# Attention of a second layer: keys and values of heads 2 to 7 as chained seven-product blocks, and another placing of the first layer's multiply-adds

## Chip, cores and metric

The kernel runs on one core of one Trainium2 chip, and the metric is the time of one execution on the device in microseconds. Lower is better. All of it is float32.

## What is computed

The reference is two networks in a row; the change lies in the second one, which has two layers. Each layer takes 256 latent tokens and 256 context tokens (512 columns in all), 1024 features wide. The part that matters is the attention inside the mixer, cut to its core:

```
ql, kl, vl, ... = in_proj_split(h_l @ w_in)      # latent tokens
qc, kc, vc, ... = in_proj_split(h_c @ w_in)      # context tokens
q, k = apply_rope(...) on latent tokens only
s = q @ k.T * 64 ** -0.5                         # two maps a head
p = softmax(s);  a = p[0] - lam * p[1];  o = a @ v
```

There are 8 heads; each has 128 columns of q, of k and of v, which are products of the tokens with a weight block of 1024 x 128. In the first layer latent and context tokens both have queries. In the second, the last, only the latent tokens have queries, while keys and values still cover all 512 tokens.

## The kernel before

**Tiles.** Tokens lie on the free axis: xnT holds the normed tokens as 8 chunks of 128 features by 512 columns, columns 0 to 255 latent, 256 to 511 context. Weights stream from HBM by DMA, issued by SyncE (SP), into 12 slots of 1024 x 128 (512 KB each). The list of tiles is fixed (weight_tiles); SP goes through it in order and waits, before each tile, until the tile 12 places earlier has been given back. A tile may be empty: it only holds a slot for sums made on the chip.

**The seven products.** Where two neighbouring weight blocks A and B (two heads, say) both meet all 512 columns, the 2 x 2 blocks (4 chunks of features by 4, 256 tokens by 256) can be done with seven products in place of eight, after sums of tokens (t1 to t4, made by DVE) and sums of weights (sums_of_weights at L896 on POOL: four TENSOR_TENSOR of 128x512 at L899 to L904, into two empty slots and over B). Each product is four matmuls of 256 columns for q and k, eight of 128 columns for v. In the first layer heads 2 to 7 are done so, and two gates of the merge: 11 jobs. The steps are named 1, 2, 6, 5, 7, 4, 3. Steps 1, 6, 7 and 4 run up a sum in PSUM bank 4 (X), and after each ScalarE (ACT) copies the bank to its quarter of q, k or v (seven_copied, L1382). Steps 2, 5 and 3 run up bank 5 (Y), and DVE adds that bank to a quarter after steps 2, 7 and 3 (seven_added, L2997 and L3000). Semaphores c_cp and c_ad count copies and adds. A product on X waits for the copy before it, a product on Y for the add before it.

**Units.** Attention runs in units s of one head and 128 queries: 32 in the first layer (4 a head), 16 in the second (2 a head; unit 2h and 2h+1 are head h). In each, PE does: scores (L2155), filler part 0, the turn (transposes, L2167) of the unit before, filler part 1, the value products (L2181) of the unit before, filler part 2. The filler is the making of q, k and v of later heads. Beside it DVE takes the maximum from PSUM (L3011), ACT two exponentials (L1390), DVE mixes the two maps in L3020 to L3025, and ACT copies the turned map (L1007), without which the value products can't start; DVE then scales the output (out_of, L3005).

**Rotation.** Latent q and k are rotated. POOL multiplies four swapped blocks of 32 rows (rotated, L932, after q and k of the head are kept and the head before is rotated), then DVE multiplies and adds (rope, L2847 and L2849), and the scores of the head wait for it. rope(h+1) stands in the last unit of head h (units 3, 7, 11, ... of the first layer; the odd ones of the second). In the second layer it stands after the mixing and before seven_added of part 1 and out_of.

**Second layer's fillers.** For head h+1, during head h, pieces (L2017) makes q (8 matmuls of 256 columns, L2029), k (8 of 512, L2038) and v (32 of 128, L2050) plainly, in 12 portions of which each part of a unit takes two. ACT keeps each whole (keep, L1283). Units 14 and 15 are filled by gates of the merge (L2194). POOL does only rotated(1) to rotated(7) there, then the weight sums of the merge, which is all of seven-product jobs.

**Multiply-adds.** Beside the first layer's attention DVE also sums rows for a later modulation: eight weight tiles of 512 KB, each in two halves of two instructions (row_sums, L2414 and L2416; a half is two instructions of 128x512). ROWS_AT lists the 16 units that take one half each, behind out_of. A tile's slot is given back with its second half. Unit 9 also has a RECIPROCAL of 512 columns (L3041), units 26, 27 and 31 token sums (L2664 to L2672).

## Time and profile before

| | |
|---|---|
| three runs | 2652.55, 2652.28, 2648.11 us; median 2652.28 |
| the profiled execution | 2652.46 us, of which the span of the trace is 2650.7 |
| PE | busy 2607.0 us, 98% |
| DVE, POOL, ACT | 1569.2, 1149.4, 786.9 us |
| chain that ended last | PE 86%, DVE 5%, issue 3%, ACT 2% |
| granted PE clock | 0.996 of full speed |
| first layer's attention, units 4 to 31 | about 878 to 1085 us |
| second layer's attention, all units | about 2108 to 2281 us |

Times are of one profiled execution, in us from the start of its span. A busy PE is not a PE at its peak, since the ends of matmuls are modelled; so lengths of work on PE are read from one start to the next. Each float32 matmul of the program shows as two of PE in the trace.

### The profile page before, as it was taken

Reading aid. Unit: us, or ns where it says so; the run is one execution under the profiler, and the core shown is the slowest. Engines: PE = TensorE matmul, PEld = TensorE weight load, DVE = VectorE, ACT = ScalarE, POOL = GpSimd, SP = SyncE. Lnnn points to the kernel's source line nnn. Section 1 sums busy time; section 2 is a strip of 40 time slices with the busy share of each in tenths; the row PEclk is TensorE's granted clock in tenths of the full one; section 3 lists DMA queues with packets and bytes.
Section 4 is the critical chain, followed back from the end, with each engine's and each line's share of the span. In section 5 each row is a group of like instructions: output and inputs, shape, how many; then the busy total and the mean of one; then the engine's idle time right before and its main releaser. Section 6 shows DMA issues by size and latency. Waiting matters only on the chain.

```text
span 2650.7 us, 39911 instructions
## 1 busy us (share of the span) xinstructions
PE 2607.0 (98%) x15266; PEld 2036.9 (77%) x15266; DVE 1569.2 (59%) x2636; ACT 786.9 (30%) x1812; POOL 1149.4 (43%) x918
## 2 busy tenths in 40 slices
PE   8999999999999999999999999999999999999998
PEld 6779995555555777888778888876666677899998
DVE  1447835777778577767869660126766733666253
ACT  2430103665656333200021210014555422201210
POOL 4018870333323544455425553401221222586885
PEclk9999999999999999999999999999999999999999
DMA  9437667434441132234455522264443321377553
GB/s 284 97 112 201 186 195 181 110 90 112 106 109 42 55 96 72 71 97 120 120 159 175 159 88 88 87 180 121 109 112 98 96 72 56 84 219 215 167 170 118
DMA packets 519310, 333.10 MB, mean 126 GB/s; under 512 B 15328, under 2 KB 485712, under 8 KB 518864
## 3 DMA queue, kind: packets, MB, share of 16 engines
q1 hardware_dynamic: 507888, 298.19, 39.9%
q0 software_dynamic: 10784, 31.46, 4.9%
q8 instruction: 122, 2.00, 0.3%
q10 hardware_dynamic: 448, 0.89, 0.1%
q14 instruction: 68, 0.56, 0.1%
HBM read 328.11 MB, written 2.38 MB: 125 GB/s over the span
## 4 chain that ended last, share of the span: by engine, by line
PE 86%; DVE 5%; issue 3%; ACT 2%; DVEq 1%; POOL 1%; PEld 1%; POOLq 1%; DMA 0%; PEldq 0%; ACTq 0%
PE ps L1859 42%; PE ps L1495 23%; PE ps L2216 2%; PE ps L2013 2%; PE ps L2038 2%; PE ps L2050 2%; PE ps L1990 1%; PE ps L2029 1%; PE ps L2181 1%; PE ps L2155 1%; PE ps L2320 1%; POOL TMP L932 1%; PE ps L1815 1%; DVE TMP L3011 1%; PE ps L1976 0%
## 5 line engine op out<-in xcount | busy, mean ns | idle before, releaser
L1495 PE MATMUL ps<-xnT,W 128*128 128x512 f32 (+1 forms) x1760 | 651.6, 526 | 1.6 <-DVE TMP L2793 0.9
L1495 PEld LDWEIGHTS ps<-xnT,W 128*128 128x128 f32 x1760 | 330.8, 191 | 290.6 <-issue 261.2
L1859 PE MATMUL ps<-TMP,W 128*128 128x128 f32 (+1 forms) x2848 | 482.3, 319 | 3.8 <-DVE TMP L2660 1.7
L899 POOL TENSOR_TENSOR W<-W 128x512 f32<-128x512 f32 x148 | 209.4, 1415 | 595.7 <-DMA W<-in_w_mlp 246.2
L1859 PEld LDWEIGHTS ps<-TMP,W 128*128 128x128 f32 x2848 | 422.9, 191 | 35.8 <-issue 2.4
L1859 PE MATMUL ps<-BIG,W 128*128 128x128 f32 (+1 forms) x2736 | 437.6, 314 | 0.7 <-DVE TMP L2700 0.5
L1859 PEld LDWEIGHTS ps<-BIG,W 128*128 128x128 f32 x2736 | 391.4, 191 | 27.8 <-issue 1.0
L1859 PE MATMUL ps<-xnT,W 128*128 128x128 f32 (+1 forms) x2032 | 324.2, 311 | 0.0
L1859 PEld LDWEIGHTS ps<-xnT,W 128*128 128x128 f32 x2032 | 288.7, 191 | 18.9 <-issue 0.6
L1007 ACT ACTIVATE TMP<-ps 128x512 f32<-128x512 f32 (+3 forms) x217 | 97.8, 457 | 621.8 <-PE ps L1859 409.3
L901 POOL TENSOR_TENSOR W<-W 128x512 f32<-128x512 f32 x148 | 210.4, 1422 | 25.6 <-issue 4.7
L902 POOL TENSOR_TENSOR W<-W 128x512 f32<-128x512 f32 x148 | 216.4, 1462 | 0.0
L904 POOL TENSOR_TENSOR W<-W 128x512 f32<-128x512 f32 x148 | 202.2, 1366 | 21.6 <-issue 0.9
L2793 DVE SCALAR_TENSOR_TENSOR TMP<-ps,prmT,TMP 128x510 f32<-128x510 f32 (+3 forms) x256 | 181.6, 714 | 43.3 <-ACT TMP L1230 28.9
L956 POOL TENSOR_TENSOR BIG<-BIG,TMP 128x512 f32<-128x512 f32 x80 | 103.8, 1312 | 226.9 <-ACT BIG L1272 226.9
L2699 DVE TENSOR_TENSOR TMP<-TMP,ps 128x128 f32<-128x128 f32 (+1 forms) x89 | 29.5, 331 | 282.9 <-PE ps L1859 273.3
L2829 DVE SCALAR_TENSOR_TENSOR TMP<-TMP 128x128 f32<-128x128 f32 x384 | 162.5, 494 | 41.6 <-ACT TMP L1266 41.6
L2416 DVE SCALAR_TENSOR_TENSOR TMP<-W,cact,TMP 128x512 f32<-128x512 f32 x140 | 176.5, 1292 | 6.8
L967 POOL TENSOR_TENSOR TMP<-TMP 128x512 f32<-128x512 f32 (+1 forms) x30 | 30.0, 999 | 280.8 <-ACT TMP L1280 278.7
L1256 ACT ACTIVATE TMP<-BIG,TMP 128x128 f32<-128x128 f32 x384 | 116.8, 389 | 1.5 <-PE ps L2013 1.5
L932 POOL TENSOR_TENSOR TMP<-TMP,cst 32x512 f32<-32x512 f32 x40 | 51.9, 1298 | 131.9 <-ACT TMP L1007 122.7
L1390 ACT ACTIVATE TMP<-ps,TMP 128x512 f32<-128x512 f32 (+1 forms) x96 | 58.3, 612 | 152.5 <-DVE TMP L3011 152.5
(388 smaller groups left out, 3315.2 us busy)
## 6 DMA issues: line engine op xcount, KB each, us to landing
W<-in_w_in SPq DMA_DIRECT2D x188, 512.0 KB, 4.2
W<-in_w_mlp SPq DMA_DIRECT2D x128, 512.0 KB, 4.0
W<-in_ada_w SPq DMA_DIRECT2D x96, 512.0 KB, 4.2
BIG<-cs_rows POOLq DMA_DIRECT2D x96, 256.0 KB, 4.8
W<-in_w_ssd_o SPq DMA_DIRECT2D x32, 512.0 KB, 4.5
W<-in_w_gate SPq DMA_DIRECT2D x22, 512.0 KB, 6.3
W<-in_w_up SPq DMA_DIRECT2D x22, 512.0 KB, 4.0
W<-in_w_down SPq DMA_DIRECT2D x16, 512.0 KB, 3.8
```

What stands on the lines that cost most here:

```text
L899: nc.gpsimd.tensor_tensor(w1[:, 0:K, :], wb[:, 0:K, :], wb[:, K:2 * K, :], ALU.add)
L901: nc.gpsimd.tensor_tensor(wb[:, 0:K, :], wa[:, 0:K, :], wb[:, 0:K, :], ALU.subtract)
L902: nc.gpsimd.tensor_tensor(w1[:, 4:4 + K, :], w1[:, 0:K, :], wa[:, 0:K, :], ALU.subtract)
L904: nc.gpsimd.tensor_tensor(w2[:, 0:K, :], wa[:, K:2 * K, :], w1[:, 4:4 + K, :], ALU.subtract).then_inc(done, 1)
L956: nc.gpsimd.tensor_tensor(e, e, xs[:, 3, ch * P:(ch + 1) * P].unsqueeze(1) .to_broadcast([P, 4, P]), ALU.mult).then_inc(ssd["ec"], 1)
L1007: return A(dst, src, ACT.Copy)
L1256: last = A(mt[:, (2 * c + d) % 4, h, :], csb[:, ch, d, h, :], ACT.Relu, scale=-1.0, bias=tabs[:, 2, ch, span(g * 4 + 32 * d + h, 1)])
L1495: last = mm(dst, w[:, c, 0:m], rhs(k), start=k == 0, stop=k == total - 1)
L1859: done = mm(PS[bank][:, third + half * H:third + half * H + H], w[:, at + c, :], x[:, c, :], start=first and opens and c == 0, stop=last a ...
L2416: last = V.scalar_tensor_tensor(out=dst, in0=w[:, k, :], scalar=c, in1=dst, op0=ALU.mult, op1=ALU.add)
L2793: last = V.scalar_tensor_tensor(out=acc[:, :, lo:hi], in0=raw[:, :, lo + k - 2:hi + k - 2], scalar=tap(l, g, t, k), in1=acc[:, :, lo:hi], ...
L2829: V.scalar_tensor_tensor(out=mt[:, c % 4, h, :], in0=mt[:, c % 4, h, :], scalar=tabs[:, 0, order[i], span(g * 4 + 32 * d + h, 1)], in1=cbm ...
```

## The change

The second layer's k and v of head pairs (2,3), (4,5) and (6,7) become six seven-product jobs; q stays plain (steps 8 and 9, one head each, 8 matmuls of 256 columns on bank X, copied by ACT). The order is written out for units 2 to 13 (the part after the colon is "part 0", "part 1", "part 2"; "2k6" is pair 2, k, step 6). Units 0 and 1 still make head 1 plainly. Waits by formula become waits by position in the written order.

```diff
+SEVEN_JOBS = ... + [(1, p, t) for p in (1, 2, 3) for t in "qkv"]
+ {2: ("1q8 1q9", "1k1 1k2 1k6", "1k5 1k7"), 3: ("1k4 1k3", "1v1 1v2", "1v6 1v5"), 4: ("1v7", "1v4", "1v3"),
+  5: ("2q8", "2q9", "2k1 2k2"), 6: ("2k6", "2k5", "2k7"), 7: ("2k4 2k3", "2v1", "2v2"),
+  8: ("2v6", "2v5", "2v7"), 9: ("2v4 2v3", "3q8", "3q9"), 10: ("3k1 3k2", "3k6 3k5", "3k7"),
+  11: ("3k4 3k3", "3v1", "3v2"), 12: ("3v6", "3v5", "3v7"), 13: ("3v4", "3v3", "")}
-ROWS_AT = (7, 8, 10, 11, 12, 13, 15, 16, 17, 18, 20, 21, 22, 23, 25, 26)
+ROWS_AT = (8, 9, 10, 12, 13, 14, 16, 17, 18, 20, 21, 22, 24, 25, 26, 28)
```

POOL makes the weight sums of k before rotated(h) and those of v after it, for h = 1, 3, 5, in both layers now (in the first, q before and k and v after):

```diff
-                    if l == 0 and h % 2 == 1 and h < 7:
+                    if h % 2 == 1 and h < 7:
                         pool.drain()
-                        sums_of_weights(seven_keys(job_for(h + 1, "q")), 4, c_ws)
+                        sums_of_weights(seven_keys(job_for(l, h + 1, "k" if l else "q")), 4, c_ws)
                         pool.drain()
                     rotated(h)
...
-                        for t in "kv":
-                            sums_of_weights(seven_keys(job_for(h + 1, t)), 4, c_ws)
+                        for t in "v" if l else "kv":
+                            sums_of_weights(seven_keys(job_for(l, h + 1, t)), 4, c_ws)
```

Waits of PE, in scores, values and the products (copies_until and adds_until count the copies or adds up to a step in the written order):

```diff
                     if qt == 0 and paired(l, h):
-                        pe.wait_ge(c_ad, 3 * job_for(h, "k") + 3)
+                        pe.wait_ge(c_cp, copies_until(job_for(l, h, "k"), 4))
+                        pe.wait_ge(c_ad, adds_until(job_for(l, h, "k"), 3))
...
-                        pe.wait_ge(c_cp, 4 * job_for(h, "v") + 4)
-                        pe.wait_ge(c_ad, 3 * job_for(h, "v") + 3)
+                        pe.wait_ge(c_cp, copies_until(job_for(l, h, "v"), 4))
+                        pe.wait_ge(c_ad, adds_until(job_for(l, h, "v"), 3))
...
+                    if step in (1, 6, 7, 4, 8, 9):
+                        pe.wait_ge(kept["att"], 6 * l + 6)
+                        if copies_until(job, step) > 1:
+                            pe.wait_ge(c_cp, copies_until(job, step) - 1)
+                    elif adds_until(job, step) > 1:
+                        pe.wait_ge(c_ad, adds_until(job, step) - 1)
```

DVE makes the second layer's token sums t1 (in unit 0), t2 and t4 (unit 1) and t3 (unit 2), each 128x1024, t1 to t4 in columns of hT and other memory that this layer does not use; the gates of units 14 and 15 wait for all copies and adds. The tile list has two empty tiles more for each of the six jobs.

```diff
-                    if l == 0 and s < 3:
+                    for _ in range((1, 2)[s] if l and s < 2 else 1 if not l and s < 3 else 0):
                         next(seven_sums, None)
```

## Rows read from the trace of the kernel before

**Rows 1.** The page: its span.

```profile
span 2650.7 us, 39911 instructions
```

**Rows 2.** Busy time by engine, second layer's units 0 to 13; last PEclk, DMA share, GB/s.

```profile
2109.00:2266.00 157.00, 157.00 (x886) 113.47 (x882) 54.28 (x96) 42.00 (x117) 38.60 (x32) 1.00 0.22 60
```

**Rows 3.** Timeline of PE, a second-layer odd unit: start, us, instructions xcount [idle before <-releaser].

```profile
2162.44 1.13 PE L2155 MATMUL ps<-TMP 64*128 64x512 f32 x4
2163.50 3.70 PE L2038 MATMUL ps<-xnT,W 128*128 128x512 f32 x8
2167.03 0.60 PE L2167 MATMUL ps<-cst,TMP 128*128 128x128 f32 x4
2167.47 3.74 PE L2050 MATMUL ps<-W,xnT 128*128 128x128 f32 x32
2171.04 1.06 PE L2181 MATMUL ps<-TMP 128*128 128x128 f32 x8
2171.94 3.74 PE L2050 MATMUL ps<-W,xnT 128*128 128x128 f32 x32
2175.60 1.13 PE L2155 MATMUL ps<-TMP 64*128 64x512 f32 x4
```

**Rows 4.** Timeline of PE, first layer: a product of q or k, then of v.

```profile
893.20 1.89 PE L2216 MATMUL ps<-xnT,W 128*128 128x256 f32 x8
894.92 0.60 PE L2167 MATMUL ps<-cst,TMP 128*128 128x128 f32 x4
...
919.70 2.05 PE L2213 MATMUL ps<-W,BIG 128*128 128x128 f32 x16
921.59 0.38 PE L2167 MATMUL ps<-cst,TMP 128*128 128x128 f32 x2
```

**Rows 5.** Timeline of ACT, second layer: the latent tokens' copy, the second exponential.

```profile
2158.22 0.38 ACT L1286 ACTIVATE TMP<-ps 128x256 f32<-128x256 f32 x1 [0.88 <-PE ps L2029]
...
2165.55 0.68 ACT L1390 ACTIVATE TMP<-ps,TMP 128x512 f32<-128x512 f32 x1
```

**Rows 6.** Timeline of DVE, second layer: maximum, mixing, rotation; last two beside POOL's weight sums.

```profile
2163.61 1.23 DVE L3011 TENSOR_REDUCE TMP<-ps 128x2 f32<-128x1024 f32 x1 [3.56 <-PE ps L2155]
...
2166.89 0.75 DVE L3025 SCALAR_TENSOR_TENSOR TMP<-TMP 128x512 f32<-128x512 f32 x1
...
2173.92 0.69 DVE L2849 TENSOR_TENSOR TMP<-TMP 128x512 f32<-128x512 f32 x1
...
2264.51 1.60 DVE L2849 TENSOR_TENSOR TMP<-TMP 128x512 f32<-128x512 f32 x1
...
2266.29 1.49 DVE L2667 TENSOR_TENSOR BIG<-xnT,BIG 128x512 f32<-128x512 f32 x1
```

**Rows 7.** Timeline of POOL: first weight sums of two sets (first layer), rotated rows (second).

```profile
1004.06 1.26 POOL L899 TENSOR_TENSOR W<-W 128x512 f32<-128x512 f32 x1 [7.97 <-PE ps L2216]
...
1055.79 2.09 POOL L899 TENSOR_TENSOR W<-W 128x512 f32<-128x512 f32 x1 [8.21 <-DVE hT L2416]
...
2167.91 5.21 POOL L932 TENSOR_TENSOR TMP<-TMP,cst 32x512 f32<-32x512 f32 x4 [17.42 <-ACT TMP L1007]
```

**Rows 8.** Timeline of PE, first layer: four waits at value products; the merge's third product.

```profile
924.34 0.71 PE L2181 MATMUL ps<-TMP 128*128 128x128 f32 x4 [0.59 <-ACT TMP L1007]
...
939.34 1.16 PE L2181 MATMUL ps<-BIG,TMP 128*128 128x128 f32 x8 [1.07 <-ACT TMP L1007]
...
982.31 0.71 PE L2181 MATMUL ps<-BIG,TMP 128*128 128x128 f32 x4 [1.85 <-ACT TMP L1007]
...
1039.51 0.71 PE L2181 MATMUL ps<-TMP 128*128 128x128 f32 x4 [1.68 <-ACT TMP L1007]
...
1088.85 1.89 PE L1859 MATMUL ps<-TMP,W 128*128 128x256 f32 x8
```

**Rows 9.** Timeline of DVE, first layer: reciprocal, multiply-adds.

```profile
933.85 3.34 DVE L3041 RECIPROCAL TMP<-TMP 128x512 f32<-128x512 f32 x1
...
976.70 2.67 DVE L2416 SCALAR_TENSOR_TENSOR hT<-W,cact,hT 128x512 f32<-128x512 f32 x2
```

More of the change, by code:

```diff
@@ L299, in seven_keys, with seven_of, steps_until, copies_until @@
         pair = [("att", l, 2 * p + i, t) for i in range(2)]
-    return pair + [("sevensums", l, p, t, k) for k in range(2)]
-def seven_of(s, part):
-    return [(SEVEN_JOBS.index((0, int(x[0]), x[1])), int(x[2])) for x in SEVEN_FILL.get(s, ("",) * 3)[part].split()]
+    return pair if (l, t) == (1, "q") else pair + [("sevensums", l, p, t, k) for k in range(2)]
+def seven_of(l, s, part):
+    return [(SEVEN_JOBS.index((l, int(x[0]), x[1])), int(x[2])) for x in SEVEN_FILL[l].get(s, ("",) * 3)[part].split()]
+SEVEN_ORDER = [x for l in range(2) for s in sorted(SEVEN_FILL[l]) for part in range(3) for x in seven_of(l, s, part)]
+def steps_until(kinds, job, step):
+    return sum(x[1] in kinds for x in SEVEN_ORDER[:SEVEN_ORDER.index((job, step)) + 1])
+def copies_until(job, step):
+    return steps_until((1, 6, 7, 4, 8, 9), job, step)
+def adds_until(job, step):
+    return steps_until((2, 5, 3), job, step)
+def copies_of(l):
+    return sum(x[1] in (1, 6, 7, 4, 8, 9) for x in SEVEN_ORDER if SEVEN_JOBS[x[0]][0] <= l)
+def adds_of(l):
+    return sum(x[1] in (2, 5, 3) for x in SEVEN_ORDER if SEVEN_JOBS[x[0]][0] <= l)
 MIXER = ["A0q", "A0k"] + list(WIDE) + [f"A{_i}{_t}" for _i in (1, 2, 3) for _t in "qkv"]
@@ L426, in weight_tiles @@
                     col(("dt", l), wi, SSD_DT, 64)
-        for h in range(8 if l else 2):
+        for h in range(2):
             for n, t in enumerate("qkv"):
@@ L758, in seven_done @@
             if step in (1, 2, 7):
-                eng.wait_ge(c_pe, 3 * job + (1, 2, 7).index(step) + 1)
+                eng.wait_ge(c_pe, steps_until((1, 2, 7), job, step))
+            elif step in (8, 9):
+                made(eng, seven_keys(job)[step - 8])
             else:
@@ L2201, in product_of @@
                     t = SEVEN_JOBS[job][2]
+                    if step in (1, 6, 7, 4, 8, 9):
+                        pe.wait_ge(kept["att"], 6 * l + 6)
[3 more added lines that the diff above has]
+                        pe.wait_ge(c_ad, adds_until(job, step) - 1)
+                    X, Y = PS[4][:, 0:S], PS[5][:, 0:S]
+                    if step in (8, 9):
+                        key = seven_keys(job)[step - 8]
+                        w = tile(key)
+                        for c in range(KC):
+                            last = mm(X, w[:, c, :], xnT[:, c, 0:nt], start=c == 0, stop=c == KC - 1)
+                        give(last, key)
+                        return
                     ka, kb, k1, k2 = seven_keys(job)
@@ L2220, in product_of @@
                     if step == 1:
-                        if job == 0:
-                            pe.wait_ge(kept["att"], 6)
-                        else:
-                            pe.wait_ge(c_cp, 4 * job)
                         tile(ka)
@@ L2254, in filled @@
                     h = us[s][0]
-                    if l == 0 and h:
-                        for job, step in seven_of(s, part):
+                    if h and (l == 0 or h < 7):
+                        for job, step in seven_of(l, s, part):
                             product_of(job, step)
@@ L2262, in _ @@
                 for s, (h, qt, k0, nk) in enumerate(us):
-                    if qt == 0 and (l or h == 0):
-                        ahead = pieces(h + 1) if h < 7 else gate_pieces(0)
+                    if qt == 0 and h == 0:
+                        ahead = pieces(1)
+                    if l and qt == 0 and h == 7:
+                        ahead = gate_pieces(0)
                     scores(s)
@@ L2986, in seven_added @@
                 def seven_added(s, part):
-                    for job, step in seven_of(s, part) if l == 0 else ():
+                    for job, step in seven_of(l, s, part):
                         if step not in (2, 7, 3):
@@ L2991, in seven_added @@
                         seven_done(dve, job, step)
-                        dve.wait_ge(c_cp, 4 * job + {2: 1, 7: 3, 3: 2}[step])
+                        dve.wait_ge(c_cp, copies_until(job, {2: 1, 7: 7, 3: 6}[step]))
                         i, m = {2: (0, 0), 7: (1, 1), 3: (0, 1)}[step]
@@ L3013, in _ @@
                     seven_added(s, 0)
-                    if l == 0 and s == 4:
+                    if s == (2 if l else 4):
                         next(seven_sums, None)
```

68 lines of the change are left out of this document (31 added, 37 removed), and 15 rows, old and new, of the table SEVEN_FILL.

## The prediction

> **What bounds the kernel now.** I read the page first: a span of 2650.7 us [rows 1], most of it PE. Then the busy time by stretch over the units that change: PE has work in all 157 us, DVE in 54, ACT in 42, POOL in 39, at the full granted clock [rows 2]. So in the second layer's attention only fewer columns on PE can save time, and only as long as nothing else makes PE wait. Then PE's timeline, for lengths from start to start. An odd unit runs 13.16 us: scores 1.06, half a k 3.53, the turn 0.44, half a v 3.57, value products 0.90, half a v 3.66, with no wait [rows 3]. So a head's k costs 7.06 and its v 7.23; a pair costs 14.12 and 14.46. The time outside the span in that execution is 1.76 us; its 2652.46 us lies 0.2 above the median of the three runs, 2652.28, so I forecast the median from it directly. Something like 0.2% (5.3 us) is what a measurement of this kernel can tell from no change.
>
> **What the products save.** A product of a k job takes 1.72 us, of a v job 1.89 [rows 4]; behind a change of shape or another product these move by some 0.1 either way, so I take 1.77 and 1.83. Seven make 12.4 and 12.8 in place of 14.12 and 14.46, which is 1.7 + 1.65 = 3.35 a pair and **10.1 us** for three. The q steps have the shapes of before: nothing. New empty tiles bring no DMA; weights of each pair land units ahead, since slots come free with the products of the pair before, and I cost them at nothing: the cover is two units or more, over 15 us.
>
> **What the chain costs.** Each unit now has its own clock. Against a unit's start [rows 3, 5, 6]: DVE's maximum starts at 1.17 and ends 2.40; ACT's second exponential ends at 3.79 and with reading its sum ACT is free at about 3.8, so a copy (0.38) ends at 4.15 at the earliest; DVE's mixing ends at 5.2. Before, ACT copied one k or v in this time; now up to three copies stand in it, and PE stands behind them where two X products have no Y product between.
>
> Unit 2, "1q8 1q9". DVE's token sums t2 and t4 now stand behind rope(1) and ahead of unit 2's maximum, while POOL makes the weight sums of 1v, a set of four such instructions of 1.26 [rows 7], over 5 us. A sum of 512 columns beside POOL took 1.49 [rows 6]; one of 1024 is more than that and less than twice it: 2.0. Both then delay the maximum by about 3.4 against a scores' end where it was waiting: the maximum starts some 4.5 into the unit, the copy of 1q8 comes 3.0 later, at 7.5, and 1q8 had ended at 4.6. **2.9** (ends: 0.6, the copy alone, and 4).
>
> Unit 4, "1v7" and "1v4": 1v7 ends at 2.95, the turn at 3.4, the copy at 4.15: **0.85** with the semaphores. In unit 5 2q9 stands behind 2q8 with only the turn between: 0.2. Other X pairs have 1.7 us of other work between them: nothing, and 0.2 for all.
>
> Rotation. k is kept by ACT at 4.15 in units 3, 7 and 11 (before: at 5.4, since k ended at 4.6). POOL's rotated takes 5.2 [rows 7] and ends at 9.45. rope takes 1.46 alone (0.69 twice and the drain [rows 6]) and 2.37 with POOL's weight sums beside its second multiply, 1.60 in place of 0.69 [rows 6]. Behind rotated(2) POOL goes at once to the sums of 2k, behind rotated(4) to those of 3k; behind rotated(6) it has rotated(7), which waits for rope(6). So the head is rotated at 11.85 in units 3 and 7 and at 10.95 in unit 11. Now the units' lengths, with scores, turn and values 2.4 in sum: unit 3 has six products, 13.3; units 7 and 11 four ("2k4 2k3", "2v1", "2v2"), 9.7. Scores of head 4 wait **2.2**, those of head 6 **1.3**. Unit 3 is long enough, but 1v5 waits for the add of 1v2, which DVE has behind rope(2): 12.3 against 11.45, **0.85**. Unit 5, 9: rotated is early, nothing. The collision of rope(1) makes head 1 0.9 later, of which 0.1 shows.
>
> Unit 13. Its value products are of head 6 and wait for 3v's last add (step 3), which is multiplied just before them, in part 1. On DVE that add stands behind rope(7). PE is ready at 5.2; DVE ends the mixing at 5.2, rope(7) at 6.6, the add at 7.0: **1.85**. Were POOL's first merge sums beside it, 1 to 2 more; by their slots they end by 4 in unit 13.
>
> Sum: 2.9 + 0.85 + 0.2 + 0.2 + 2.2 + 1.3 + 0.85 + 0.1 + 1.85 = **10.4**. The second layer's attention comes out level, +0.3. After it nothing moves: POOL begins the merge's sums as the slots allow, as before.
>
> The Trainium skill (SBUF — State Buffer, section "Who interferes with whom") says that a vector instruction with two SBUF inputs and a GpSimd one that reads SBUF take one shared port as an exclusive lock, and the loser waits out the whole other instruction. The 0.91 us lost [rows 6] are under one instruction of 1.26 [rows 7], so the trace agrees. By that rule t2 and t4 could each wait out 1.26, and unit 2's term would be 3.7 in place of 2.9.
>
> **The first layer.** The halves leave units 7, 11, 15 and 23 and go to 9, 14, 24 and 28. There a half (2.67 beside POOL [rows 9]; alone two instructions of some 0.7, as rope's [rows 6]) stood ahead of the next unit's maximum, and the value products waited for ACT's copy: 0.59 us in unit 8, 1.85 in unit 16, 1.68 in unit 24 [rows 8]. I take all three as gone: -4.1. The unit 11 one showed no wait. In unit 9 the half joins a RECIPROCAL of 3.34 [rows 9] that already makes 1.07 of wait at 939.34 [rows 8]: +1.4. In 14 and 24 DVE has slack; in 28 POOL no longer runs beside it (its sums wait for the slot that this half gives back), so about 0. Weight tiles for which SP waits behind those slots come one unit later (about 8 us), the last two units, 15 us: the merge's first sums, which wait for the last of these slots, began at 1055.8 [rows 7], and PE first uses them at 1088.9 [rows 8]; moved 15 and 5 long, they are still made 12 ahead: nothing. POOL's sums fall on other instructions of DVE: -1 to +2, taken as 0. Net **-2.7**, ends -4.5 and +1.5.
>
> **Total:** 2652.46 + 0.3 - 2.7 = **2650.0**.
>
> **Rivals.**
> 1. Faster: the waits overlap. If the maximum of unit 2 is not held by t2 and t4 (0.6), the rotations are alone (1.3 and 0 in units 7 and 3) and the add comes in time in unit 13 (0.5), the sum is 0.6 + 0.85 + 0.4 + 1.3 + 1.3 + 0.1 + 0.5 = 5.0, and the time 2652.46 - 10.1 + 5.0 - 2.7 = 2644.7. For it: every term is a difference of two chains that I laid out from another unit's rows. Against: in the first layer just such chains made waits [rows 8]. Chance 0.30.
> 2. Slower: the shared port. DVE and POOL hold each other up in both layers. It decides where POOL's sums overlap all of rope, each multiply losing the 0.91 [rows 6]: then units 3 and 7 have 0.9 more each, 11 and 13, where I left POOL out, 1.8 each, unit 2 1, and the moved sums in the first layer eat up its 2.7. Sum 6.4 + 2.7: 2659.1. Against: POOL starts its sums only after DVE's first multiply has begun, and behind rotated(6) it has none to make. Chance 0.11.
> 3. The second layer does as forecast and the first layer's placing brings nothing, since the reciprocal of unit 9 and the half in 28 give back what units 16 and 24 gain: 2652.8. Chance 0.12.
> 4. No wait remains at all, the whole 10.1 + 2.7: 2639.7. The copy behind 1q8 and the add ahead of head 6's values speak flatly against it. Chance 0.03.
> My forecast keeps 0.44.
>
> **How the numbers follow.** Faster by over 0.2% (under 2647.0) are rivals 1 and 4, less a tail of 1 (0.04), plus 0.03 of the forecast: 0.32. Slower (over 2657.6) is most of rival 2 and a small tail of 3: 0.11. Within: 0.57. The likeliest case alone would have 2647 to 2654. The range for 8 in 10 runs from 2643, which takes in rival 1 with a margin of 2 for its terms, to 2656.
>
> **What would show it.** Right: in units 2 to 13 PE's busy time falls by about 10 us and waits of near 10 appear, the largest ahead of 1q9 (line of the plain q products, released by ACT), ahead of the scores in units 8 and 12 (released by DVE's rope) and at the value products of unit 13 (released by DVE's add); in the first layer the waits at the value products of units 16 and 24 are gone and that of unit 10 grows to over 2. Wrong: waits of 5 or less in those units, or POOL's sums overlapping the first multiply of rope, or new waits of the merge for its first weight sums.

## The result, and the profile after

The changed kernel takes 2654.03 us (median of 22 executions, 2650.58 to 2659.37), the kernel before 2650.36 (22 executions, 2645.98 to 2655.37). The ratio is 1.0016, 95% interval 1.0010 to 1.0022: 4.2 us slower (2.7 to 5.8). That is under the 0.2% that I had named as the limit of a measurement, but with this many executions the interval doesn't include 1. A second set of 11 gave 1.0009 (1.0001 to 1.0018), 2.4 us. The sign is the opposite of the one that I forecast (-2.4).

The page of the changed kernel: span, busy time by engine, and the chain that ended last.

```profile
span 2652.7 us, 40131 instructions
PE 2599.8 (98%) x15290; PEld 2047.1 (77%) x15290; DVE 1606.2 (61%) x2658; ACT 788.3 (30%) x1824; POOL 1190.2 (45%) x942
PE 88%; DVE 4%; issue 3%; ACT 2%; DVEq 1%; POOL 1%; PEld 1%; POOLq 0%; PEldq 0%; DMA 0%; ACTq 0%
```

PE is 7.2 us less busy than before, and the span [rows 1] is 2.0 longer. The mean granted clock fell from 0.996 to 0.994. The windows (busy time by engine in a stretch of time) say more. They are laid from one landmark to another: the lines that end at 2290.92 and 2293.79 run from the second layer's first scores to the first product of the merge behind it, the last line of each block from the scores of unit 4 to the same product in the first layer. Columns: length, PE, PEld, DVE, ACT, POOL busy, then the granted clock, the DMA share and GB/s. First the kernel before:

```profile
2108.58:2290.92 182.34, 180.43 (x1012) 132.13 (x1011) 69.98 (x120) 52.35 (x144) 48.77 (x38) 1.00 0.21 58
878.83:1084.95 206.12, 195.30 (x1151) 158.76 (x1151) 139.81 (x224) 69.90 (x241) 95.88 (x71) 1.00 0.26 74
```

and the kernel after:

```profile
2109.00:2266.00 157.00, 147.54 (x896) 121.45 (x894) 80.11 (x112) 43.76 (x129) 79.77 (x58) 0.99 0.24 66
2107.04:2293.79 186.75, 174.86 (x1036) 142.57 (x1035) 96.71 (x142) 54.08 (x156) 85.35 (x62) 0.98 0.23 63
876.67:1082.14 205.47, 196.25 (x1151) 159.96 (x1151) 141.91 (x224) 69.85 (x241) 99.09 (x71) 0.99 0.26 74
```

The first line answers to [rows 2]: where PE had work in all 157 us, it now sits idle for 9.5, and DVE's and POOL's work has grown from 54 and 39 us to 80 each. The second layer's stretch is 4.41 us longer, the first layer's 0.65 shorter. Together +3.76. The spans of the two profiles differ by only 2.0, because outside these stretches, where PE's work is the same, the changed kernel's profile is 1.8 shorter: 2.2 ahead of the first layer's unit 4 and 0.9 behind the second layer, less 1.3 between the two. The executions gave 4.2 and, in the second set, 2.4; I take 3.76 as what the change did in this pair of profiles.

Where PE waits in the second layer (timeline of PE, the lines with idle time before them, and one without; in brackets the us and what ended them). Lines after the change: L2185 is the scores, L2211 the value products, L2244 the plain q, L2258 and L2261 the products of v and of k, L2885 rope's last instruction, L3036 the add.

```profile
2129.33 1.13 PE L2185 MATMUL ps<-TMP 64*128 64x512 f32 x4 [0.48 <-DVE TMP L2885]
2136.68 3.69 PE L2244 MATMUL ps<-xnT,W 128*128 128x256 f32 x16 [2.57 <-issue]
2163.19 2.05 PE L2258 MATMUL ps<-W,hT 128*128 128x128 f32 x16 [1.13 <-DVE BIG L3036]
2165.17 1.13 PE L2185 MATMUL ps<-BIG 64*128 64x512 f32 x4
2169.47 2.02 PE L2258 MATMUL ps<-W,BIG 128*128 128x128 f32 x16 [0.75 <-ACT BIG L1411]
2207.40 2.08 PE L2185 MATMUL ps<-TMP 64*128 64x512 f32 x4 [2.58 <-DVE TMP L2885]
2252.61 1.13 PE L2185 MATMUL ps<-BIG 64*128 64x512 f32 x4 [1.67 <-DVE BIG L2885]
2267.72 1.13 PE L2211 MATMUL ps<-BIG,TMP 128*128 128x128 f32 x8 [1.83 <-DVE BIG L3036]
```

These are the waits that the prediction laid out, nearly one by one. That of 2136.68, ahead of 1q9, the profile puts down to "issue"; what stands ahead of it is ACT's copy of 1q8 (timeline of ACT), which ends at 2136.58:

```profile
2136.20 0.38 ACT L1411 ACTIVATE BIG<-ps 128x256 f32<-128x256 f32 x1
```

But the scores at 2207.40 took 2.08 us where [rows 3] and the line at 2252.61 have 1.13. The windows around them, and around the wait of the first layer's unit 10, show why (last columns again clock, DMA share, GB/s):

```profile
2205.00:2207.40 2.40, 0.00 (x0) 0.00 (x0) 2.33 (x3) 0.00 (x0) 2.00 (x2) 1.00 0.00 0
2207.40:2209.40 2.00, 2.00 (x4) 0.51 (x4) 1.95 (x3) 0.00 (x0) 2.00 (x2) 0.51 0.00 0
2209.40:2212.00 2.60, 2.60 (x19) 2.59 (x18) 1.22 (x1) 1.21 (x3) 2.21 (x3) 0.72 0.00 0
2268.70:2270.70 2.00, 2.00 (x6) 0.45 (x4) 0.95 (x2) 0.00 (x0) 1.86 (x2) 0.54 0.00 0
936.00:938.00 2.00, 0.47 (x2) 0.47 (x3) 1.16 (x3) 2.00 (x8) 1.19 (x1) 0.92 1.11 343
938.00:940.00 2.00, 2.00 (x10) 1.72 (x10) 1.93 (x3) 0.04 (x1) 1.86 (x3) 0.50 0.30 75
```

Behind the wait PE is granted 0.5 of its speed, the lower of its two levels (1.2 in place of 2.4 GHz), and is back at full speed some 3.5 us later. What PE's work loses follows from the rows: 2.00 x 0.49 + 2.60 x 0.28 = 1.7 us. The kernel's time can lose less, when a wait that stood behind gets shorter by it. There are three such stretches in the changed attention (938, 2207, 2269) and none in that of the kernel before.

That is no chance of one profile. Every execution comes with its mean granted clock: over the 22 of the changed kernel it averages 0.9941, over the 27 of the kernel before that were timed beside the last experiments 0.9960. 0.0019 of 2650 us is 5.0 us, three stretches of 1.7. How much of that reaches the time is another question: within each kernel, over the 231 executions whose clock is on record, 0.001 of mean clock goes with some 1.8 us and not with 2.65 (an estimate; the clock is rounded to 0.001, which makes it a little too low).

### The profile page after: what moved, and what is told of

Its sections match the earlier page's. It is cut to its first block, busy times and chain, and to the rows that moved or that the text cites. A ratio compares the mean times of both kernels' runs of the same rounds, so it can differ in the third digit from the quotient of the medians.

```text
span 2652.7 us, 40131 instructions
## 1 busy us (share of the span) xinstructions
PE 2599.8 (98%) x15290; PEld 2047.1 (77%) x15290; DVE 1606.2 (61%) x2658; ACT 788.3 (30%) x1824; POOL 1190.2 (45%) x942
## 4 chain that ended last, share of the span: by engine, by line
PE 88%; DVE 4%; issue 3%; ACT 2%; DVEq 1%; POOL 1%; PEld 1%; POOLq 0%; PEldq 0%; DMA 0%; ACTq 0%
PE ps L1888 42%; PE ps L1524 23%; PE ps L2261 3%; PE ps L2042 2%; PE ps L2258 2%; PE ps L2019 1%; PE ps L2185 1%; PE ps L2211 1%; POOL TMP L961 1%; PE ps L2244 1%; PE ps L2356 1%; PE ps L2058 1%; PE ps L1844 1%; PE ps L2079 1%; PE ps L2067 1%
## 5 line engine op out<-in xcount | busy, mean ns | idle before, releaser
L928 POOL TENSOR_TENSOR W<-W 128x512 f32<-128x512 f32 x154 | 216.9, 1408 | 624.2 <-DMA W<-in_w_mlp 243.2
L1036 ACT ACTIVATE TMP<-ps 128x512 f32<-128x512 f32 (+3 forms) x205 | 91.1, 449 | 579.4 <-PE ps L1888 408.5
L930 POOL TENSOR_TENSOR W<-W 128x512 f32<-128x512 f32 x154 | 219.5, 1425 | 26.8 <-issue 5.2
L931 POOL TENSOR_TENSOR W<-W 128x512 f32<-128x512 f32 x154 | 226.3, 1470 | 0.0
L933 POOL TENSOR_TENSOR W<-W 128x512 f32<-128x512 f32 x154 | 212.1, 1377 | 22.5 <-issue 0.9
L1259 ACT ACTIVATE TMP<-ps,prmT 128x512 f32<-128x512 f32 x64 | 41.8, 653 | 181.1 <-PE ps L1524 181.1
```

What stands on the lines that cost most here:

```text
L928: nc.gpsimd.tensor_tensor(w1[:, 0:K, :], wb[:, 0:K, :], wb[:, K:2 * K, :], ALU.add)
L930: nc.gpsimd.tensor_tensor(wb[:, 0:K, :], wa[:, 0:K, :], wb[:, 0:K, :], ALU.subtract)
L931: nc.gpsimd.tensor_tensor(w1[:, 4:4 + K, :], w1[:, 0:K, :], wa[:, 0:K, :], ALU.subtract)
L933: nc.gpsimd.tensor_tensor(w2[:, 0:K, :], wa[:, K:2 * K, :], w1[:, 4:4 + K, :], ALU.subtract).then_inc(done, 1)
L1036: return A(dst, src, ACT.Copy)
```

## The experiments

My theory was that the forecast waits of the second layer, together with the half clock behind some of them, eat up what the products save. The rivals: the new placing of the multiply-adds costs, or something outside the attention does, through the added work of POOL and DVE. Differences in us below are the ratio's distance from 1 times 2650.

### products_only: the second layer alone

```diff
-ROWS_AT = (8, 9, 10, 12, 13, 14, 16, 17, 18, 20, 21, 22, 24, 25, 26, 28)
+ROWS_AT = (7, 8, 10, 11, 12, 13, 15, 16, 17, 18, 20, 21, 22, 23, 25, 26)
```

> The changed kernel with the first layer's multiply-adds put back in their old units; the second layer's seven products stay. Theory W (waits and clock): in the profile of the changed kernel the second layer's attention, from its first scores to the merge's first product, took 186.75 us against 182.34, because waits of some 11 us and two stretches at half the granted clock behind them (3.3 us) ate the 10.1 us of products. Then this kernel is slower than before by about 4.4 us (2 to 6). Rival P (placing): the loss comes from the moved multiply-adds, by the wait of 2.57 us in unit 10 and the half clock behind it; then this kernel is faster than before, by up to 10 us, and in no case slower. Rival E (extra work elsewhere: more instructions, slots and POOL sums): slower by some us, but with the second layer's attention itself no longer than before.

Measured: 1.0013 (1.0004 to 1.0022), +3.4 us (1.1 to 5.8). So the loss sits in the second layer. Its windows, second layer and then first:

```profile
2107.57:2292.52 184.95, 172.05 (x1037) 141.12 (x1036) 98.13 (x142) 53.81 (x156) 85.28 (x62) 1.00 0.23 63
878.53:1084.02 205.49, 194.79 (x1151) 158.89 (x1151) 139.41 (x224) 69.95 (x241) 95.40 (x71) 1.00 0.26 74
```

This execution met no half clock in the attention, although the wait of 2.57 us at the scores of unit 8 is there, and its second layer takes 2.61 us more than before: idle time +10.99, busy time -8.38. The changed kernel's stretch, and that of rows_mix below, which has both half clocks too, is 186.75: 1.80 us more. So two stretches of half clock, 3.4 us of PE's work, cost 1.80 of time here: 1.31 from the scores of unit 8 to those of unit 12, and only 0.48 from unit 14's scores on, since unit 14's value products wait 0.97 in this profile and not at all behind the half clock.

### places_only: the first layer alone

The kernel before with the new ROWS_AT, the reverse of the diff above.

> The kernel before with the new placing of the first layer's multiply-adds and nothing else. Theory W: units 4 to 31 of the first layer took 0.6 us less in the profile of the changed kernel than before, with waits gone in units 8, 16 and 24 (4.1 us) and new ones in units 10 and 27 (2.6 us) plus about 1.6 us at half clock behind unit 10's. So -0.6 us, and -2.2 where the clock does not fall behind unit 10. Rival P: slower than before by 3 us or more.

Measured: 0.9997 (0.9988 to 1.0006), -0.8 us (-3.2 to +1.6). The first layer's stretch is 204.74 us against 206.12. It doesn't cost, so the placing isn't what makes the kernel slower. It doesn't bring the 2.7 either, and its profile shows where that went: the wait of unit 10 grew to 2.57, as forecast, but with half clock behind it, and the value products took 2.07 in place of 1.16 [rows 8]; and near 1057 there is a wait of 1.83 that was not forecast.

```profile
937.84 2.07 PE L2181 MATMUL ps<-BIG,TMP 128*128 128x128 f32 x8 [2.57 <-ACT TMP L1007]
```

### tsums_early: t1, t2 and t4 made behind the mixing of units 0 and 1

```diff
+                    for _ in range((2, 1)[s] if l and s < 2 else 0):
+                        next(seven_sums, None)
                     if s == 0:
                         dve.wait_ge(ssd_sum, l + 1)
...
-                    for _ in range((1, 2)[s] if l and s < 2 else 1 if not l and s < 3 else 0):
+                    for _ in range(1 if not l and s < 3 else 0):
```

> The changed kernel with the second layer's token sums t1, t2 behind the mixing of unit 0 and t4 behind that of unit 1, where DVE waited for others, and not ahead of unit 2's maximum. Theory W: the wait ahead of 1q9 falls from 2.57 us to about 0.6 (the copy alone), and the time by 2 us against the changed kernel, so to about +1.7 against the kernel before. Rival E: the wait goes and comes back in the next units, time as the changed kernel's, +3.7.

Measured: 1.0002 (0.9993 to 1.0010), +0.5 us (-1.9 to +2.7); below the +1.7, which the interval holds. The wait ahead of 1q9 went from 2.57 to 0.52, so t2 and t4 did make it, and head 1's scores wait 1.27 in place of 0.48, because t1 and t2 now stand ahead of unit 1's maximum. Timeline of PE:

```profile
2131.67 1.13 PE L2185 MATMUL ps<-TMP 64*128 64x512 f32 x4 [1.27 <-DVE TMP L2885]
2136.97 3.26 PE L2244 MATMUL ps<-xnT,W 128*128 128x256 f32 x14 [0.52 <-issue]
```

### rope7_early: head 7 rotated in unit 12

```diff
-                    if h < 7 and qt == nq - 1 and (l == 1 or h == 1):
+                    if h < 7 and qt == nq - 1 and (l == 1 and h < 6 or h == 1) or l == 1 and s == 12:
```

> The changed kernel with the rotation of head 7 on DVE moved from unit 13 to unit 12, so that the last add of pair 3's v no longer stands behind it. Theory W: the wait of 1.83 us at unit 13's value products falls to about 0.5, and if the half clock behind it (scores of unit 14 in 1.95 us instead of 1.06, the next product in 2.58 instead of 1.83) came from that wait, it goes as well, another 1.65: together 3.0 us less than the changed kernel, about +0.7 against the kernel before. If the half clock has nothing to do with that wait it stays, and the gain is 1.3. Rival E: no gain, +3.7.

Measured: 1.0023 (1.0013 to 1.0032), +6.1 us (3.4 to 8.5). A miss, in the wrong direction. Earlier, the rotation lay beside POOL's weight sums for the merge, and unit 12's DVE work with it. Timeline of DVE, both instructions of rope (0.69 each when alone):

```profile
2256.77 1.75 DVE L2883 TENSOR_TENSOR BIG<-BIG,cst 128x512 f32<-128x512 f32 x1
2258.60 1.60 DVE L2885 TENSOR_TENSOR BIG<-BIG,TMP 128x512 f32<-128x512 f32 x1
```

Unit 13's maximum, mixing and last add came later, and the wait at unit 13's value products was 3.40 in place of 1.83, with a double stretch of half clock that began 1.3 us before the wait was over. Moving a late step forward helps only if nothing that holds it up runs there.

### add_first: seven_added of part 1 ahead of rope

```diff
+                    if l:
+                        seven_added(s, 1)
                     if h < 7 and qt == nq - 1 and (l == 1 or h == 1):
                         rope(h + 1)
-                    seven_added(s, 1)
+                    if l == 0:
+                        seven_added(s, 1)
```

> The changed kernel with DVE's adds of part 1 ahead of the rotation in the second layer's units, not behind it. Theory W: the wait ahead of 1v5 in unit 3 (1.13 us) goes, since DVE idles before the rotation there; in unit 13 the add ends at about 5.7 after the unit's start and the rotation at 7.1, so 1.83 becomes 0.5 at the value products and 0.5 at unit 14's scores. 2.0 us less than the changed kernel, and up to 1.6 more if the half clock in unit 14 goes with the wait: +0.6 to +2.2 against before. Rival E: no gain, +4. Moving the rotation to unit 12 instead cost 2 us: POOL's merge sums then held DVE up, and the add came later still.

Measured: 0.9997 (0.9988 to 1.0006), -0.8 us (-3.2 to +1.6), better than expected, since this execution met no half clock behind unit 13. The wait of 1v5 (1.13) is gone and unit 13's is 0.72 in place of 1.83 (timeline of PE):

```profile
2266.86 1.13 PE L2211 MATMUL ps<-BIG,TMP 128*128 128x128 f32 x8 [0.72 <-DVE BIG L3036]
```

So the add of step 3 did stand behind rope(7), as the prediction had it.

### pool_apart: POOL's weight sums wait for the rotation

```diff
+                        if l:
+                            pool.wait_ge(roped, 8 * l + h)
                         sums_of_weights(... "k" ...)
...
+                        if l:
+                            pool.wait_ge(roped, 8 * l + h + 1)
                         for t in "v" if l else "kv":
```

> The changed kernel with POOL's weight sums of the second layer held back until DVE has done the rotation that they ran beside (rope(1), rope(2), rope(4) and the two after). Theory W with the shared port: the second multiply of those rotations takes 0.69 in place of 1.60, so the waits ahead of unit 8's scores fall from 2.58 to 1.7, ahead of 1v5 from 1.13 to 0.2, of unit 2's from 0.48 to 0; DVE's t2 and t4 still run beside the sums. About 2.2 us less than the changed kernel, and 1.6 more where unit 8 has half clock: 0 to +2 against before. Rival S (it was not the port but the place of the rotation): no change in the multiply's length, no gain.

Measured: 0.9997 (0.9988 to 1.0006), -0.8 us (-3.2 to +1.6). In the changed kernel rope's second instruction of head 4 ran beside POOL's first weight sum. Timeline of DVE there:

```profile
2204.99 0.69 DVE L2883 TENSOR_TENSOR TMP<-TMP,cst 128x512 f32<-128x512 f32 x1 [2.48 <-POOL TMP L961]
2205.75 1.59 DVE L2885 TENSOR_TENSOR TMP<-TMP 128x512 f32<-128x512 f32 x1
```

and in pool_apart:

```profile
2204.04 0.69 DVE L2887 TENSOR_TENSOR TMP<-TMP,cst 128x512 f32<-128x512 f32 x1 [2.48 <-POOL TMP L961]
2204.81 0.69 DVE L2889 TENSOR_TENSOR TMP<-TMP 128x512 f32<-128x512 f32 x1
```

The wait of unit 8 fell by just these 0.9 us, to 1.67, and no half clock followed. The POOL instruction beside the slow one, in the changed kernel, ran from 2205.26 to 2206.80 (timeline of POOL):

```profile
2205.26 1.54 POOL L928 TENSOR_TENSOR W<-W 128x512 f32<-128x512 f32 x1 [0.31 <-issue]
```

The loss of 0.9 is under its 1.54 us. By the Trainium skill's exclusive lock (SBUF — State Buffer, section "Who interferes with whom") the instruction that comes second waits until the first is done; the trace agrees, since DVE's was done 0.54 us after POOL's.

### refilled: another order of the steps

```diff
-  2: ("1q8 1q9", "1k1 1k2 1k6", "1k5 1k7"), 3: ("1k4 1k3", "1v1 1v2", "1v6 1v5"), 4: ("1v7", "1v4", "1v3"),
-  5: ("2q8", "2q9", "2k1 2k2"), ... 7: ("2k4 2k3", "2v1", "2v2"),
+  2: ("1q8", "1q9", "1k1 1k2 1k6 1k5 1k7"), 3: ("1k4 1k3", "1v1", "1v2 1v6"), 4: ("1v5", "1v7", "1v4"),
+  5: ("1v3 2q8", "2q9", "2k1 2k2"), ... 7: ("2k4 2k3", "2v1", "2v2 2v6"),
...
-  11: ("3k4 3k3", "3v1", "3v2"), 12: ("3v6", "3v5", "3v7"), 13: ("3v4", "3v3", "")}]
+  11: ("3k4 3k3", "3v1", "3v2 3v6"), 12: ("3v5", "3v7", ""), 13: ("3v4", "3v3", "")}]
```

> The changed kernel with the same products in another order of parts: no two products on bank X side by side without other work between (1q8 in part 0, 1q9 in part 1), and units 3, 7 and 11 with five products (11.5 us) where the rotation takes 11.9. Theory W: waits ahead of unit 8's scores 0.4 in place of 2.58, unit 12's 0 in place of 1.67, 1q9 about 2 in place of 2.57, 1v5 0; 1v7|1v4 0; the wait of unit 13 stays at 1.8 with its half clock. 6 us of waits less than the changed kernel, and 1.6 more where unit 8 had half clock: -2 to -4 against before. Rival E: the waits move into other units and the time stays at +4.

Measured: 0.9999 (0.9991 to 1.0008), -0.3 us (-2.4 to +2.1); 3 us short of the middle of what I expected. The longer units 7 and 11 hide most of the rotations (head 4's scores wait 0.79 in place of 2.58, head 6's no longer; head 2's now wait 0.79), but unit 12 is now so short that unit 13's value products wait 4.09 for the add behind rope(7), with a double stretch of half clock that begins in the wait. Timeline of PE:

```profile
2265.14 2.04 PE L2211 MATMUL ps<-BIG,TMP 128*128 128x128 f32 x8 [4.09 <-DVE BIG L3036]
```

### all_parts: tsums_early, add_first, pool_apart and refilled together, and one multiply-add moved

```diff
-ROWS_AT = (8, 9, 10, 12, 13, 14, 16, ...
+ROWS_AT = (8, 10, 11, 12, 13, 14, 16, ...
```

> All of it: products reordered, token sums early, adds of part 1 ahead of the rotation, POOL's sums held back, and in the first layer the multiply-add of unit 9 (beside the reciprocal) put back into unit 11. Theory W: the second layer's attention has waits of about 2 to 3 us in place of 11 and no half clock, so it takes 182.3 - 10.1 + 2.5 - 1.2 = 173.5 us in place of 186.7; the first layer gains 1.5 of wait and 1.6 of half clock against the changed kernel. Against before: -8.8 - 2.5 = -11, with -7 to -13 as the range. Rival E: the seven products bring nothing even without waits: -2 or so.

Measured: 0.9960 (0.9947 to 0.9973), 10.6 us faster than the kernel before (7.2 to 14.0): faster than both kernels. Windows of its profile, second layer and first:

```profile
2105.45:2284.62 179.17, 174.10 (x1037) 142.65 (x1035) 94.02 (x142) 54.43 (x156) 86.93 (x62) 0.98 0.24 65
878.49:1080.63 202.14, 194.62 (x1151) 159.07 (x1151) 140.06 (x224) 69.96 (x241) 98.71 (x71) 1.00 0.27 75
```

Second layer 3.17 us under before, first 3.98: 7.2 in all, and its span is 7.7 us shorter [rows 1]. This profiled execution, at a mean clock of 0.994, is the slowest of the six; the other five have 0.996 to 0.997 and spans of 2636.2 to 2640.1. The 10.6 of the runs would be the 7.2 with some two stretches of half clock (3.4) fewer than this profile has; no profile of a faster execution was taken that would show it. PE's idle time in the second layer is 5.07 us in place of the changed kernel's 11.89. What is left is mostly unit 13 (timeline of PE), two waits in a row with a double stretch of half clock, which takes 3.0 us of PE's work:

```profile
2256.27 1.13 PE L2215 MATMUL ps<-BIG,TMP 128*128 128x128 f32 x8 [1.72 <-DVE BIG L3040]
2258.31 2.08 PE L2189 MATMUL ps<-BIG 64*128 64x512 f32 x4 [0.91 <-DVE BIG L2889]
```

### second_parts: the same without the moved multiply-add

all_parts with the change's own ROWS_AT.

> The kernel after with the four edits of all_parts to the second layer, and the first layer's multiply-adds where the change put them. By the landmarks of all_parts the second layer takes 179.3 us from its first scores to the merge against 182.3 before, and by those of the change the first layer 205.5 against 206.1: 3.7 us below the kernel before, range 1.5 to 7. The distance to all_parts is the worth of the one moved multiply-add in the first layer: 3.3 us by the landmarks. If all_parts gained mostly elsewhere, this run comes out within 1.5 us of it.

Measured: 0.9980 (0.9971 to 0.9988), -5.3 us (-7.7 to -3.2), 1.6 more than expected and inside the range. all_parts stands 5.3 below it where 3.3 was expected; the two were timed in different sets, all_parts with six executions. The four edits to the second layer together are worth 8 to 10 us against the changed kernel; singly they had come out 4 to 5 below it, which doesn't add up. A reading, not a test: the profile of each single edit also lacks one or two of the three stretches of half clock, and each can go only once.

### rows_mix: only the moved multiply-add

The changed kernel with the ROWS_AT of all_parts.

> The kernel after with one multiply-add of the first layer moved from unit 9 to unit 11 (places 8, 10, 11, 12, 13, 14, ...). The wait of the values' products in unit 10 should fall from 2.57 us to 1.07, and the half clock behind it be gone: 1.5 plus 0 to 1.6 us, so 1.5 to 3.3 us below the kernel after, and within -1 to +3 us of the kernel before. If the wait of unit 10 is no matter (something later in the first layer sets the end), it equals the kernel after.

Measured: 0.9995 (0.9986 to 1.0003), -1.3 us (-3.7 to +0.8), 3.4 us below the changed kernel timed beside it (2650.70 and 2654.10). The wait of unit 10 is back at 1.06 and the products behind it at 1.16 (timeline of PE):

```profile
933.36 1.16 PE L2211 MATMUL ps<-BIG,TMP 128*128 128x128 f32 x8 [1.06 <-ACT TMP L1036]
```

The first layer's stretch is 202.16 us against the changed kernel's 205.47. So one half of a multiply-add behind the RECIPROCAL in unit 9 cost 3.3 us: 1.5 of wait, and 1.8 by the half clock and by what moved with it.

### waits_added: only waits, in the kernel before

```diff
                     dve.drain()
+                    if l and h in (3, 4, 5, 6):
+                        V.reciprocal(hT[:, 0:2, S:T], hT[:, 0:2, S:T])
+                        dve.drain()
```

> The kernel before, with one reciprocal of 512 columns (about 3.3 us by the row of the first layer's) put on VectorE into the rotation of heads 3 to 6 of the second layer, on data that nothing reads any more. Nothing else is changed: TensorE has the same products as before, and the chained seven are not in it. The scores of units 6, 8, 10 and 12 should each come to wait about 2.4 us for the rotation. If a wait costs its length alone, the time is 4 x 2.4 = 9.6 us above the kernel before, and the granted clock stays at 1.00 behind the waits. If TensorE is put at half clock behind some such waits, each of those costs about 1.6 us more: 11 to 16 us above, with stretches of 0.50 in the granted clock at one or more of the four places, and scores of 2.0 us in place of 1.1. If the clock falls only because of the chained products' own pattern of work, no such stretch is seen here.

Measured: 1.0050 (1.0035 to 1.0065), +13.3 us (9.3 to 17.2), the case with half clock; 9.6 alone is just inside the interval. This is the run that tells the clock from the products: the kernel before has no chained products in the second layer. The four waits (timeline of PE):

```profile
2186.00 2.08 PE L2155 MATMUL ps<-TMP 64*128 64x512 f32 x4 [2.43 <-DVE TMP L2852]
2214.28 1.13 PE L2155 MATMUL ps<-TMP 64*128 64x512 f32 x4 [2.42 <-DVE TMP L2852]
2239.42 1.24 PE L2155 MATMUL ps<-TMP 64*128 64x512 f32 x4 [2.42 <-DVE TMP L2852]
2266.19 1.13 PE L2155 MATMUL ps<-TMP 64*128 64x512 f32 x4 [2.42 <-DVE TMP L2852]
```

and windows: from 2184 on around the first of them, and the whole stretch of the second layer.

```profile
2184.00:2186.00 2.00, 0.00 (x0) 0.00 (x0) 1.93 (x3) 0.21 (x1) 0.00 (x0) 0.92 0.53 117
2186.00:2192.00 6.00, 6.00 (x14) 3.67 (x15) 3.02 (x6) 1.45 (x4) 0.00 (x0) 0.50 0.16 48
2192.00:2194.00 2.00, 2.00 (x12) 1.82 (x11) 0.15 (x1) 0.60 (x1) 0.00 (x0) 0.87 0.00 0
2116.48:2315.22 198.74, 187.18 (x1012) 136.39 (x1011) 83.39 (x124) 52.65 (x144) 48.73 (x38) 0.97 0.20 53
```

The stretch is 16.40 us longer than before: 9.65 of idle time, which is four waits, and 6.75 of busy time, with the same 1012 matmuls. Three of the four waits had half clock behind them, the first 3.3 us' worth (6.00 x 0.50 + 2.00 x 0.13; it began 0.3 before the wait was over), the third and fourth 1.7 each: 6.7. So waits alone do it, without chained products, and with no other wait behind them that could take it up, the time loses all of it. The profiled execution was the longest of the five, 10 us over the other four, at a clock of 0.993; its span is 23.3 us longer than before's, 6.9 of them outside this stretch, which the added waits don't explain; over all five the mean clock is 0.9944, 0.0016 under the kernel before's, which is 4.2 us. With 9.65 of waits that makes 13.9, and 13.3 was measured.

### after_again: the changed kernel once more

> The kernel after once more, beside the other three on one chip: 4.2 us above the kernel before by the 22 runs of each (2.7 to 5.8). In its profile the waits of 2.6 us in unit 8 and 1.8 us in unit 14 of the second layer and 2.6 us in unit 10 of the first stand at the same places; a stretch of half clock follows some of them. If the three stretches of the first profile are fixed by the program, they are at the same three places again; if not, one or two are missing, and those scores take 1.1 us.

Measured: 1.0009 (1.0001 to 1.0018), +2.4 us (0.3 to 4.8). The waits and all three stretches of half clock are at the same places, and its landmarks lie 186.75 and 205.40 us apart. But products_only and tsums_early had none behind unit 8's wait of 2.57. The program sets where it can happen, not fully where it does.

## Why the prediction was wrong

The account of the two stretches, in us against the kernel before. Idle and busy time are those of profiles that run the same program in the stretch and met no half clock there: products_only for the second layer, refilled for the first, whose window is

```profile
880.26:1084.68 204.42, 194.84 (x1151) 158.93 (x1151) 138.92 (x224) 69.94 (x241) 100.40 (x71) 1.00 0.26 74
```

What the changed kernel's own profile has on top is the cost of the half clock.

```
                 idle of PE   busy of PE   without half clock   half clock    sum
second layer      +10.99        -8.38           +2.61             +1.80      +4.41
first layer        -1.24        -0.46           -1.70             +1.05      -0.65
together           +9.75        -8.84           +0.91             +2.85      +3.76
forecast           +7.7        -10.1            -2.4                0        -2.4
```

**The step that failed** first is one that the prediction never took: it priced a wait at its own length. Nothing in the sum, the bounds or the rivals stood for PE's clock; I had read 1.00 in [rows 2] and not asked what it would be once PE waited. The three stretches took 5.1 us of PE's work and cost 2.85 us of time, the largest part of the 6.2 between -2.4 and +3.76. (The first layer's 1.05 is rough: eight profiles of the same placing with the half clock have 204.74 to 205.60 us, the one without it 204.42.) But the clock is not what turns the sign: without it the account is +0.91, which is still 3.3 above the forecast. That is the second step that failed, a term of the sum too large: of these 3.3 the products, saving less than I had put down, are 1.7, the second layer's waits 0.6, and the first layer 1.0. [Rows 8] could not warn of the clock, since no wait there up to 1.85 us was followed by such a stretch.

The Trainium skill (TensorE: Matmul & The Clock Gate, section "Part 1: The HAM clock gate") gives two levels for this clock; the granted clock of 1.00 and of 0.50 to 0.51 agrees. It also says that how many matmuls run slow differs from run to run of one kernel; here two profiles of the changed kernel had the same three stretches in the attention, while the mean clock of its executions goes from 0.992 to 0.996. For the ramp (the slow first matmuls) it names a penalty under 1% of a typical span. By that figure alone the clock would have passed as nothing to count; the 2.85 us here are 0.1% of the span, and more than the gain that I forecast.

**The products** were mis-sized: 8.45 in units 2 to 13 (135.85 us of busy time before, 127.40 in products_only) against 10.1. Seven k products take 12.36, as forecast. Seven v products take 13.1 from start to start, waits taken out, where I had 12.8: [rows 4] has 1.89 for a v product, and I took 1.83. With 1.89 the sum would have been 8.8. The rest I didn't locate.

**The waits of the second layer** were right in the main: 10.7 us idle in units 2 to 13, in place of 10.35 forecast there.
- 1q9 in unit 2: 2.57 for 2.9. DVE's sums t2 and t4 stand where I put them; the timeline of DVE has t2 (L3006) at 1.85 and t4 (L3009) at 2.12, both beside POOL's sums, and t3 (L3012) at 1.21 alone:

```profile
2129.63 1.85 DVE L3006 TENSOR_TENSOR hT<-xnT,hT 128x1024 f32<-128x1024 f32 x1
2131.58 2.12 DVE L3009 TENSOR_TENSOR BIG<-xnT,hT 128x1024 f32<-128x1024 f32 x1
2133.62 1.21 DVE L3047 TENSOR_REDUCE TMP<-ps 128x2 f32<-128x1024 f32 x1
2134.75 1.21 DVE L3012 TENSOR_TENSOR xnT<-xnT 128x1024 f32<-128x1024 f32 x1
```

  I took 2.0 for each. By the Trainium skill's lock, as the prediction read it, each would wait out 1.26 and take 2.47, and the wait, an estimate, would be 2.9 + 2 x 0.47 = 3.8 (the prediction has 3.7); the trace stays below that.
- 1v5 behind the add of 1v2: 1.13 for 0.85. 1v4 behind the copy of 1v7: 0.75 for 0.85. Head 4's scores: 2.58 for 2.2. Head 6's: 1.67 for 1.3. Unit 13's value products: 1.83 for 1.85. Head 1: 0.48 for 0.1.
- What the forecast called no wait was none, and no product waits for a weight tile. 2q9 starts 0.69 after the turn before it where 0.44 is the rule [rows 3]: 0.25, for 0.2.

**The first layer** was forecast at -2.7 and gave -0.65. The waits of units 8, 16 and 24 are gone, and unit 10's grew by 1.5, all as said. Two things were missed. Half clock behind unit 10's wait took some 1.05. And 1.1 of the gain came back at 1057.50, where the wait is 1.83 in place of 0.69: behind POOL's moved sums, unit 27's scaling and mixing on DVE took 1.00 and 1.41. I had put such shifts at -1 to +2 and taken 0. Timelines of PE and of DVE there:

```profile
1057.50 0.71 PE L2211 MATMUL ps<-BIG,TMP 128*128 128x128 f32 x4 [1.83 <-ACT TMP L1036]
```

```profile
1049.37 1.00 DVE L3058 SCALAR_TENSOR_TENSOR TMP<-TMP,small 128x1 f32<-128x1 f32 x1
1050.45 1.41 DVE L3061 SCALAR_TENSOR_TENSOR TMP<-TMP 128x256 f32<-128x256 f32 x1
```

**The rivals.** Rival 1 (overlapping waits) fell: the waits came in full. Rival 2, the only one clearly slower, came out with the sign right and the mechanism mostly wrong: POOL's sums met rope's first multiply once (head 5, 1.75 us at 2224.63), and no wait stood behind it; pool_apart took away the overlap there is with the second, and unit 8's wait moved by 0.9. Its last part, that POOL's moved sums eat up the first layer's gain, came true for the 1.1 us at 1057.50. Rival 3 was nearest in time (2652.8, +0.3) and half right: the first layer did bring little. Rival 4 was ruled out by the same waits.

**What stays open.** How the half clock's cost would come out over many profiles: 2.85 rests on one or two profiles of each kind. And why the wait of unit 2 never had half clock behind it (eight profiles) and that of unit 8, as long, mostly had. No experiment tried to steer it.

## What to carry to other kernels

On this kernel, whose PE is 98% busy, saving columns by chaining products traded 8.8 us of PE time for 9.8 of waits, since the links had too little other work between them; lay out the chain with the new unit lengths first, and refill the order until the gaps are gone (all_parts: edits that singly came out level with the kernel before, together 0.4% ahead). Price a longer wait of PE at more than its length: read the granted clock in the windows behind each, since 1.7 us or more of PE's work was lost behind 25 of the 64 waits of 1.66 us and over in the table below, and ask whether a later wait takes part of it up, as here (2.85 of 5.1). Where a row of the trace has the very product that you are pricing, take its number. And an edit judged alone can look worthless because it uncovers the next wait, as refilled did with unit 13.

## What the runs showed of the hardware

- Stretches of half clock (0.50 of full, 1.2 GHz) behind short waits of PE in an otherwise full stretch, each worth 1.7 us of PE's work, sometimes two in a row (up to 3.4; less where the stretch began while PE still waited). Waits of over 1 us in the attention of all 14 profiled executions, by place:

```
place                                  wait, us         waits   followed by half clock
first layer, unit 10                   2.57 to 2.58       9             8
second layer, unit 8, scores           2.57 to 2.58       7             5
second layer, unit 2, 1q9              2.13 to 2.57       8             0
waits_added, four scores               2.42 to 2.43       4             3
unit 13, values (changed order)        1.82 to 1.83       6             4
all_parts, second_parts, unit 13       1.72, then 0.9     2             2 (3.0 us each)
rope7_early, refilled, unit 13         3.40, 4.09         2             2 (2.7 us each)
second layer, unit 12, scores          1.67 to 1.68       8             0
pool_apart, unit 8, scores             1.67               1             0
first layer, near 1057                 1.83 to 1.84      11             0
first layer, near 982, 1040            1.66 to 1.85       6             1
any place                              1.0 to 1.3        all            0
```

  Length alone doesn't decide, and none of those under 1.7 us was followed.
- Stretches of the same length show elsewhere too, near 400, 1365 and 1767 us, in most profiles of either kernel. The one near 1365 is in the changed kernel's profile and not in that of before, but places_only and waits_added, which have the second layer of before, have it too: so it doesn't come from the second layer's products. Executions of one kernel differ in clock: among the 22 of the changed kernel the mean goes from 0.992 (2659.4 us) to 0.996 (2650.6 and 2652.6 us).
- DVE and POOL beside each other: two inputs of 512 columns 0.69 us alone, 1.59 to 1.75 beside POOL's sums; the token sums of 1024 columns (t1, t2, t4) 1.85 to 2.29 beside them, where t3 alone took 1.21. The mixing's last instruction (L3061), which neither the prediction nor the account has as a term, took 0.75 alone and 1.67 to 1.81 beside POOL, in 8 of the second layer's 16 units of the changed kernel.
